# Two language-model blocks on one core: the norm behind an expert stage, the order of products behind turned tiles, and where roots are taken

## The reference, cut to what matters

```
for l in range(2):
    p = x @ w_in[l]                        # q, k, v, r, a_low, u, v_sgu
    h = concat(gla(q, k, v, r, a_low), sgu(u, v_sgu)) @ w_out[l]
    x = layer_norm(a * x + h)
    h = softmax(x @ wq @ (mem @ wk).T / 16) @ (mem @ wv) @ wo   # by head
    x = layer_norm(a * x + h)
    h = sum_e gate[:, e] * ((silu(x @ w_gate[e]) * (x @ w_up[e])) @ w_down[e])
    x = layer_norm(a * x + h)
h = rms_norm(x);  proj = h @ w_in_2
x = x + (sig(ga) * (attention @ w_out_a) + sig(gb) * (scan @ w_out_b)) @ w_out_2
x = x + experts(rms_norm(x))               # top 2 of 16, as above
x = x + sig(x @ w_ple_gate) * (p @ w_ple_proj)
out = rms_norm(x)
```

## Time and profile before

| | |
|---|---|
| median of three executions | 1800.01 us |
| profiled execution | 1798.53 us |
| its span | 1796.8 us |
| TensorE products, busy | 1549.1 us (86%) |
| VectorE, busy | 1311.1 us (73%) |
| ScalarE, busy | 1120.5 us (62%) |
| GpSimd, busy | 32.7 us (2%) |
| read from HBM | 420.15 MB |
| the chain that ended last | TensorE 41%, VectorE 31%, ScalarE 20% |

### The profile page before, as it was taken

One profiled execution on the slowest core, in us unless ns is written; L12 is line 12 of the kernel. 1 busy time (PEld: TensorE's weight loads), 2 busy tenths in 40 slices (PEclk: granted clock), 3 DMA queues, 4 the chain that ended last, 5 costly groups with the idle time before them and its releaser, 6 DMA issues.

```text
span 1796.8 us, 20954 instructions
## 1 busy us (share of the span) xinstructions
PE 1549.1 (86%) x7971; PEld 1290.1 (72%) x7971; DVE 1311.1 (73%) x1784; ACT 1120.5 (62%) x1335; POOL 32.7 (2%) x67
## 2 busy tenths in 40 slices
PE   7899858999995989977999996688996679999975
PEld 6788747788874778855777874676885557788854
DVE  4756476999995577455999997557655568999963
ACT  5444428998992544524989995256553358889952
POOL 4000000000001000000000000000000000000000
PEclk9999979999996999987999998889997899999988
DMA  9345346999994435433999997244433349999940
GB/s 332 123 167 186 103 154 221 375 380 366 384 382 164 141 141 194 141 114 116 379 367 374 380 385 267 79 133 141 141 117 105 135 155 357 367 369 378 392 184 24
DMA packets 176693, 422.76 MB, mean 235 GB/s; under 512 B 7052, under 2 KB 7216, under 8 KB 176576
## 3 DMA queue, kind: packets, MB, share of 16 engines
q1 hardware_dynamic: 172400, 407.92, 63.2%
q0 software_dynamic: 4176, 13.30, 2.2%
HBM read 420.15 MB, written 1.05 MB: 234 GB/s over the span
## 4 chain that ended last, share of the span: by engine, by line
PE 41%; DVE 31%; ACT 20%; issue 6%; DMA 1%; DVEq 0%; ACTq 0%
DVE w_low L1499 18%; ACT w_high L1194 14%; PE ps L602 11%; PE ps L603 10%; PE ps L604 10%; DVE out_low L1731 3%; ACT work L1266 1%; PE ps L800 1%; PE ps L683 1%; PE ps L826 1%; PE ps L787 1%; ACT x_odd L1252 1%; PE ps L1027 1%; ACT spread L1270 1%; PE ps L1009 1%
## 5 line engine op out<-in xcount | busy, mean ns | idle before, releaser
L1499 DVE TENSOR_TENSOR w_low<-raw,w_high 128x1024 fp32r<-128x1024 f32 x588 | 694.2, 1221 | 285.8 <-ACT w_high L1194 285.1
L1194 ACT ACTIVATE w_high<-raw 128x1024 fp32r<-128x1024 f32 x588 | 599.5, 1054 | 344.8 <-PE ps L604 338.9
L602 PE MATMUL ps<-w_high,act_high 128*128 128x512 f32 x464 | 189.2, 408 | 26.2 <-issue 10.7
L603 PE MATMUL ps<-w_low,act_high 128*128 128x512 f32 x464 | 186.2, 401 | 0.0
L604 PE MATMUL ps<-w_high,act_low 128*128 128x512 f32 x464 | 185.4, 400 | 0.0
L826 PE MATMUL ps<-w_high,hT 128*128 128x512 f32 x384 | 156.0, 406 | 0.1
L826 PE MATMUL ps<-w_low,hT 128*128 128x512 f32 x384 | 155.2, 404 | 0.0
L800 PE MATMUL ps<-w_high,x_odd 128*128 128x512 f32 x384 | 152.2, 396 | 0.0
L800 PE MATMUL ps<-w_low,x_odd 128*128 128x512 f32 x384 | 150.1, 391 | 0.0
L602 PEld LDWEIGHTS ps<-w_high,act_high 128*128 128x128 f32 x464 | 90.5, 195 | 51.3 <-issue 29.2
L1499 DVE TENSOR_TENSOR w_low<-work,w_high 128x1024 fp32r<-128x1024 f32 x96 | 113.1, 1221 | 0.0
(11 more groups left out here) (354 smaller groups left out, 2847.7 us busy)
## 6 DMA issues: line engine op xcount, KB each, us to landing
raw<-in_w_up SPq DMA_DIRECT2D x96, 1024.0 KB, 7.6
raw<-in_w_gate SPq DMA_DIRECT2D x51, 1024.0 KB, 7.6
raw<-in_w_down SPq DMA_DIRECT2D x48, 1024.0 KB, 7.7
work<-in_w_gate SPq DMA_DIRECT2D x45, 1024.0 KB, 8.1
x_res<-in_w_down SPq DMA_DIRECT2D x45, 1024.0 KB, 7.3
raw<-in_w_in SPq DMA_DIRECT2D x44, 1024.0 KB, 5.8
raw<-in_w_out SPq DMA_DIRECT2D x12, 1024.0 KB, 4.8
raw<-in_wk_x SPq DMA_DIRECT2D x8, 1024.0 KB, 5.0
```

The lines of the kernel that those rows point to most:

```text
L602: pe.matmul(out, lh, rh, start=first, stop=False)
L603: pe.matmul(out, lh, rl, start=False, stop=False)
L1194: A(split_unit(n)[0], raw_unit(n), ACT.Copy).then_inc(high_ready, 1)
L1499: V.tensor_tensor(split_unit(n)[1], raw_unit(n), split_unit(n)[0].bitcast(F32), ALU.subtract).then_inc(low_ready, 1)
```

## The change

1. `layer_norm` of an expert stage's sum moves into VectorE's branch and reads the two PSUM slots of the sums; the copy by ScalarE goes. After the third stage ScalarE copies the sums straight to `x`. What follows the norm on VectorE (low parts of the next turned tiles, the RMS norm of the second block) moves into the branch as well. Of the four splits behind the last output, three go ahead of it on both engines and one behind.
2. `dense_cols`, `dense_rows` and `dense_turned` get a `head`: for the first three units they run all products with the high part of the activation (tile by tile, as each high part is there), then those with the low part. `dense_rows` for the attention's output starts so with the first half of the chunks. It is used behind ten turned operands; the narrow products (routers) run all high products first. The units of a head are released at its end.
3. `slot_gates` on VectorE comes behind `output` of the expert before, with eight splits together; three of four down chunks run ahead of `slots_turned` (before two).
4. `rsqrt` goes. VectorE signals that the variance is there, GpSimd raises it to the power -0.5 in one instruction, and VectorE waits for it where it is used. In `layer_norm` each tile has its own aggregate, addition of eps and root.
5. GpSimd's queue has the roots between its parameter loads; the load of `p_2` and of the last norm's parameters change places.

```diff
+            def root(v):
+                nonlocal roots
+                roots += 1
+                pool.wait_ge(S["var_ready"], roots)
+                nc.gpsimd.tensor_tensor(v, v, minus_half(*v.shape[1:]), ALU.pow).then_inc(S["rstd_ready"], 1)
...
             for l in range(DEPTH):
                 if l:
                     pool.wait_ge(S["normed"], TT * 3 * l)
                     load_layer(l)
-                load_norm(3 * l + 1)
-                load_norm(3 * l + 2)
-                load_norm(3 * l + 3)
+                root(v_rstd)
+                root(o_rs)
+                for k in range(3):
+                    for t in range(TT):
+                        root(rstd[:, t, :])
+                    load_norm(3 * l + k + 1)
+            root(rstd)
             load_norm(3 * DEPTH + 1)
+            root(u_rs)
             load_norm(3 * DEPTH + 2)
-            load_norm(3 * DEPTH + 3)
             pool.wait_ge(S["m2_ready"], TT)
             pool.dma_start(p_tok, ...)
+            root(rstd)
+            load_norm(3 * DEPTH + 3)
+            root(rstd)
...
-            def dense_rows(names, chunks, src=MAIN):
+            def dense_rows(names, chunks, src=MAIN, head=None, halves=None):
...
+                if head is not None or halves is not None:
+                    begun = HEAD
+                    for t in range(TT):
+                        high_made(halves[0] if halves is not None else head[t])
+                        for k in range(HEAD):
+                            unit_ready(n + k)
+                            with_high(n + k, k, t)
+                    for t in range(TT):
+                        wait_released(pe, halves[0] if halves is not None else head[t])
+                        for k in range(HEAD):
+                            i = with_low(n + k, k, t)
+                            if t == TT - 1:
+                                i.then_inc(unit_used, 1)
+                    n += HEAD
...
-                        for k in range(2):
+                        for k in range(FC - 1):
                             down(e - 1, k)
                     if e < NE:
                         pe.wait_ge(gu_copied[m], e + 1)
                         pe.wait_ge(turner_ready[m], 1)
                         slots_turned(e)
                     if 0 < e <= NE:
-                        for k in range(2, FC):
-                            down(e - 1, k)
+                        down(e - 1, FC - 1)
...
-            def layer_norm(k, src, splits=0, arrived=None):
+            def layer_norm(k, src, centred, splits=0, arrived=None):
                 for t in range(TT):
                     if arrived is not None:
                         dve.wait_ge(arrived, t + 1)
                     for b in range(2):
-                        i = V.bn_stats(bn[:, t, b, :], src[:, t, 512 * b:512 * b + 512])
-                link(i)
-                for t in range(TT):
-                    i = V.bn_aggr(mean_var[:, t, :], bn[:, t, :, :])
-                link(i)
-                link(V.tensor_scalar(rstd, mean_var[:, :, 1:2], LN_EPS, None, ALU.add))
-                rsqrt(28, TT)
+                        i = V.bn_stats(bn[:, t, b, :], src[t][:, 512 * b:512 * b + 512])
+                    link(i)
+                    link(V.bn_aggr(mean_var[:, t, :], bn[:, t, :, :]))
+                    root_inverted(V.tensor_scalar(rstd[:, t, :], mean_var[:, t, 1:2], LN_EPS, None, ALU.add))
                 split(splits)
...
+                    dve.wait_ge(S["rstd_ready"], roots - TT + t + 1)
...
             def experts(m):
...
                     experts_own(m)
+                    if m < DEPTH:
+                        finished(m, [ps[...] for s in SUM_SLOTS], sums_done[m])
+                        split(1)
...
+            def finished(m, sums, arrived):
+                layer_norm(3 * m + 2, sums, y_acc, arrived=arrived)
+                if m < DEPTH - 1:
+                    V.memset(aT, 1.0)
+                    tiles_low(act_low, act_high, (f"{m + 1}.xT0", f"{m + 1}.xT1"))
+                else:
+                    dve.wait_ge(S["normed"], TT * 3 * DEPTH)
+                    rms_norm(3 * DEPTH, x, h_tok, ...)
+                    tiles_low(act_low, act_high, ("2.xT0", "2.xT1"))
...
                     if e < NE:
-                        split(4)
-                        slot_gates(e)
-                        split(4)
+                        split(8)
+                    if e == NE:
+                        split(3)
                     if e:
                         output(e - 1)
-                split(4)
+                    if e < NE:
+                        slot_gates(e)
+                if m == DEPTH:
+                    split(1)
```

More of the change, by code:

```diff
@@ L29 @@
 SPLIT = 6
+HEAD = 3
 SLOTS = 4
@@ L625, in dense_cols @@
                         for t in range(TT):
-                            k = 2 * j + c
-                            i = three(bank[:, t, :], operand(src, k, t * P, t * P + P), weights(n, 512 * c, 512 * c + 512),
-                                      k == 0, k == KC - 1)
+                            with_high(n, 2 * j + c, t)
+                            i = with_low(n, 2 * j + c, t)
                     if j < 3:
@@ L641, in dense_rows, with with_high, with_low @@
                 last = 2 * chunks - 1
-                for k in range(2 * chunks):
+                def with_high(n, k, t):
+                    for b in range(2):
+                        wh, wl = weights(n, 512 * b, 512 * b + 512)
+                        xh = src[0][:, k, t * P:t * P + P]
+                        pe.matmul(slot_banks(names[t])[:, b, :], xh, wh, start=(k == 0), stop=False)
+                        pe.matmul(slot_banks(names[t])[:, b, :], xh, wl, start=False, stop=False)
+                def with_low(n, k, t):
+                    for b in range(2):
+                        i = pe.matmul(slot_banks(names[t])[:, b, :], src[1][:, k, t * P:t * P + P], weights(n, 512 * b, 512 * b + 512)[0],
+                                      start=False, stop=(k == last))
+                    return i
+                begun = 0
+                if head is not None or halves is not None:
+                    begun = HEAD
+                    for t in range(TT):
+                        high_made(halves[0] if halves is not None else head[t])
+                        for k in range(HEAD):
+                            unit_ready(n + k)
+                            with_high(n + k, k, t)
+                    for t in range(TT):
+                        wait_released(pe, halves[0] if halves is not None else head[t])
+                        for k in range(HEAD):
+                            i = with_low(n + k, k, t)
+                            if t == TT - 1:
+                                i.then_inc(unit_used, 1)
+                    n += HEAD
+                for k in range(begun, 2 * chunks):
                     unit_ready(n)
+                    if halves is not None and k == chunks:
+                        wait_released(pe, halves[1])
                     for t in range(TT):
-                        for b in range(2):
-                            i = three(slot_banks(names[t])[:, b, :], operand(src, k, t * P, t * P + P),
-                                      weights(n, 512 * b, 512 * b + 512), k == 0, k == last)
+                        with_high(n, k, t)
+                        i = with_low(n, k, t)
                         if k == last:
@@ L694, in turn, with narrow_turned, narrow @@
                 full(i, name)
-            def narrow_turned(name, c0, width):
+            def narrow_turned(name, c0, width, head=None):
                 begin(name)
+                dst = slot_ps(name)[0:width, 0:T]
+                if head is not None:
+                    high_made(*head)
                 for c in range(KC):
-                    i = three(slot_ps(name)[0:width, 0:T], (nar_high[:, c, c0:c0 + width], nar_low[:, c, c0:c0 + width]),
-                              operand(MAIN, c, 0, T), c == 0, c == KC - 1)
+                    pe.matmul(dst, nar_high[:, c, c0:c0 + width], act_high[:, c, 0:T], start=(c == 0), stop=False)
+                    pe.matmul(dst, nar_low[:, c, c0:c0 + width], act_high[:, c, 0:T], start=False, stop=False)
+                if head is not None:
+                    operand_ready(*head)
+                for c in range(KC):
+                    i = pe.matmul(dst, nar_high[:, c, c0:c0 + width], act_low[:, c, 0:T], start=False, stop=(c == KC - 1))
                 full(i, name)
-            def narrow(name, c0, width):
-                narrow_turned(name + "T", c0, width)
+            def narrow(name, c0, width, head=None):
+                narrow_turned(name + "T", c0, width, head)
                 begin(name)
@@ L1491, in _ @@
             turned = 0
+            roots = 0
             def split(count):
@@ L1809, in _ @@
                 link(i)
+                root_ready()
                 for t in range(TT):
@@ L1868, in _ @@
```

(2 more changed lines are left out.)

188 lines of the change are left out of this document (120 added, 68 removed).

## The result

Four executions of the changed kernel took 1707.66 to 1715.11 us, median **1709.03**, beside 1800.58 for the kernel before: ratio 0.950 (95% interval 0.947 to 0.953). The forecast was 1741 with a range of 1727 to 1762. The direction was right and the size was not: 91 us came (from the 1800.01 that the forecast started from) where 59 were expected.

The account below looks back on a forecast made before the run. TensorE bounds dense stages, four things run almost level in expert stages, and a serial chain bounds their ends. Terms 23.5 + 10.7 + 13.2 + 11.4 = 58.8 us off the profiled 1798.5; forecast 1741 beside the median, range 1727 to 1762.

Parts of the forecast that it names:

- What is late next is TensorE: 16.23 us of work an ordinary early expert.: Expert stages: with VectorE's 1.0 us wait gone, TensorE's work sets the pace; 3.8 us a stage, 11.4 in three.
- When it makes choices VectorE has 15.6 and 1.4, 17.0.: Early experts with choices: VectorE's work sets 17.0 us instead of 17.6, giving 2 x 0.6 us a stage.
- The late ones may slow.: Late experts: DMA is at its end near 400 GB/s, 15.7 against 15.59 us; 0.4 taken off each stage.
- Rival (b): Expert stages reach TensorE's own rows (18 us), round trips and second additions cost nothing: 1730 us; chance 0.10.
- Part 2: Products behind other turned tiles: starting with high parts closes four TensorE gaps, 4.8 + 2.4 + 3.4 = 10.7 us.
- The joints: Ends of the three expert stages: earlier norm, shorter roots and earlier products save 10.3, 10.0 and 3.2, together 23.5 us.
- Part 3: Roots outside the joints, moved to GpSimd: 4.7 gated unit, 4.1 ahead of routers, 4.4 RMS norms; together 13.2 us.
- Rival (d): A GpSimd power is a software loop of length R, several us; slower from R of 6, at 8 1830 us; chance 0.04.
- The rule of mutual exclusion: Two-SBUF-input VectorE passes and SBUF-reading GpSimd instructions exclude each other: 1.2 us less over two norms ahead of routers.
- The limit of about 358 GB/s: HBM limit per core: an expert's 6.29 MB would take 17.6 us and the expert-stage part would bring nothing.
- (a): Expert stages keep their pace because DMA already moves 400 GB/s: 1752 us; chance 0.20.
- (c): Joints give half, 12 instead of 23.5 us, as waits move to branch exit or unsplit weights; chance 0.06.

Follow-up runs that it names:

- e3: Changed kernel with both edits inside the expert loop undone (slot gates early, down products 2+2): 1742.9 us, beside 1798.8 for the kernel before.
- e4: Kernel before with the two expert loop edits alone (slot gates late, down products 3+1): 1767.0 us, beside 1798.8 for the kernel before.
- e5: Changed kernel with every product behind turned tiles waiting for high and low parts again, in the old order: 1735.1 us, beside 1804.1 for the kernel before.
- e6: Changed kernel with all roots back on VectorE as twelve instructions, none on GpSimd: 1734.0 us, beside 1804.1 for the kernel before.
- e11: Kernel before with only the norm in the branch, read from PSUM, and three splits ahead of the last output: 1790.2 us, beside 1801.3 for the kernel before.
- e17: The changed kernel itself, measured again: 1709.0 us, beside 1799.6 for the kernel before on the same chip.
- e15: Changed kernel with the roots of the linear attention's norm alone back on VectorE: 1709.7 us, beside 1803.8 for the kernel before.
- e16: Kernel before with products that add no result in TensorE's idle stretches at twelve places: 1789.5 us, beside 1799.6 for the kernel before.

## Why the prediction was wrong in size

Set against what taking each part back cost (or bringing it in alone), the forecast's terms are:

| part | forecast | measured |
|---|---|---|
| loop edits | 11.4 | 34 (e3), 32 (e4) |
| high parts first: 10.7 and 2.4 + 1.3 + 2.4 in the joints | 16.8 | 23 (e5) |
| roots: 13.2 and 2.0 + 2.0 in the joints | 17.2 | 20 (e6) |
| norm in the branch, from PSUM: 5.9 + 5.9, 0.8 in the third | 12.6 | 9 to 11 (e11) |

The forecast's parts make 58.0, and 58.8 with the 0.8 of the parameters' fetch. The measured ones make 84 to 88 of 91; with errors of 4 to 9 us on each, no interaction can be told. Of the 32 us beyond the forecast the loop is 21 to 23, the heads 6 and the roots 3. No run took back the new order of GpSimd's loads (5 in the change).

- **The step that failed: "What is late next is TensorE: 16.23 us of work an ordinary early expert."** This is the term of the sum that was mis-sized: 11.4 us for the three expert stages, where 32 to 34 came. The engine was named rightly and its work was taken too large, for it was read from busy time. A product's row lasts 0.39 us while the next starts 0.23 behind it; ahead of each stop the last product's tail counts as work, and behind it the first row is longer (0.53, 0.47). The start-to-start sum is 15.94. The ordinary period fell by 0.63 and not by 0.37: eight times, 5.1 and not 3.0 us a stage.
- **"When it makes choices VectorE has 15.6 and 1.4, 17.0."** Measured 16.19. A buffer of split units lies between VectorE and TensorE, so VectorE may be behind for one expert: its 4 x 15.56 + 1.43 for four experts is 15.92 an expert, just under TensorE's floor. The trace agrees (VectorE idles 0.2 us in the three experts from 361.44 to 409.49); no run tested it apart. With the stage's first period (17.36 to 16.44) that is 4.0 instead of 1.2.
- **"The late ones may slow."** They ran faster, 14.95 to 15.56 instead of 15.59, at 394 to 401 GB/s: VectorE has no idle time there, so by this account its lead lets TensorE run at its own 14.95 until the lead is used up. 1.8 instead of -0.4. The last high output came 15.55 behind the last period's start instead of 14.66, which gives back 0.9; 10.8 less 0.9 is the 9.9 of the first stage. In e17 it came 13.4 behind, after slower last periods, so what sets a stage's end stays open. In the third stage the kernel before lost some 3 us more in its first two periods (18.02 and 19.24), where the granted clock was 0.96 and 0.86. e11 has the same pair at the same clocks in its first two stages and not in the third, so this loss comes and goes in the old loop; in no stage of the new one does it stand. The slower of the two periods, in the kernel before and then in e11 (columns as in the earlier trace rows; the clock is the third figure from the end):

```profile
1486.80:1506.00 19.20, 18.63 (x83) 15.72 (x82) 15.10 (x16) 15.04 (x19) 0.00 (x0) 0.86 0.97 361
```

```profile
307.20:326.30 19.10, 18.73 (x83) 15.75 (x82) 15.19 (x16) 15.07 (x19) 0.00 (x0) 0.86 1.01 359
```

- **Rival (b)**, TensorE's own rows, named the mechanism and had the chance of 0.10; it took the same 16.2 for the floor and so stopped at 18 of 32 to 34.
- **Part 2** left out the clock: 23 against 16.8. Slow products follow at some of the places and cost some 2 us each there (rows of e5).
- **The joints** were right step by step in the first: 5.9 (measured 5.86), 2.0 (2.13), 2.4 (2.49). The second has the parameters' fetch at 3.82 in the chain and gave 9.2 of 10.0; the 0.8 of the third did not come. The norm alone came 1 to 3 low by the time, no more than its error; by e11's trace 5.2 and 5.1 for 5.9 each.
- **Part 3** was right in sum within the error, with different prices: a root takes 0.55 to 1.7, not 0.1. In the norms of summed rows and the gated unit's it is hidden as said; where it is exposed VectorE waits 0.8 and 1.2 against the 0.9. The linear attention's, costed at nothing, gave some 0.9 in the second layer (e15). Rival (d) fell: R is 0.55 to 1.5 against its deciding 6.
- **The rule of mutual exclusion** (the Trainium skill, SBUF — State Buffer, section Who interferes with whom) holds in this trace: 0.55 becomes 1.52 beside a two-input pass that began 0.16 earlier, and stays 0.55 beside one that reads PSUM. The estimate of 1.2 us lost by it was wrong, and its 0.3 a root stood on no row. The same section says that whichever starts first keeps the port, and VectorE's pass, first to start, kept its 1.28. Its next pass began at 235.80, while the root's row still lasted until 236.17, and kept its 1.28 too: a shut-out for the root's whole row does not show. The limit of about 358 GB/s (the Trainium skill, DMA: Bandwidth & Descriptors, section Where 436 GB/s comes from) does not hold here either; the last expert moved 401.
- Rivals (a), (c): neither came. What would have shown the forecast wrong from the other side, stalls behind the first three units or waits for roots in the norms of summed rows, is not in the trace.

## What to carry to other kernels

Take the floor of a pipelined engine from start-to-start times over work without a stop, never from its busy share beside a stop. Where several waits lie on one ring of engines, cost them together: each alone gave 2.4 of 10.8 us, and a buffer ahead of the floor engine averages the uneven work of the one that feeds it. Price an idle stretch of TensorE at its length plus the slow work that may stand behind it (look for it in the rows: here 0 to 3 us), and if it can't be closed, fill it with products right behind the last real one.

## What the hardware showed unexpectedly

- A gap of 2.4 to 2.6 us ahead of products is followed at some places by 7 to 14 products of 512 columns 0.43 apart instead of 0.23 (e16 at 569.16 and 766.88, before at 1363.15), and at others by none (before at 213.38 and 772.34).
- The granted clock can be low with TensorE busy throughout. The changed kernel's window in the second block (its profile, columns as above), where two later profiles of it were 7 to 10 us shorter:

```profile
1240.00:1250.00 10.00, 10.00 (x42) 7.96 (x41) 4.60 (x10) 6.06 (x5) 0.00 (x0) 0.67 0.39 151
```

- A power on GpSimd of 128x1 takes 0.55 us, 128x8 1.65; where it must wait for VectorE's pass, GpSimd's row grows (1.52) and VectorE's pass keeps its 1.28.
